# Two decoder blocks in one kernel: gate and up as seven block products, and the down products spread between the tiles of the next group

## Chip, cores and metric

The kernel runs on one core of one Trainium2 chip. The metric is the device time in microseconds (us), the median of the runs. Engines: PE (TensorE matmul) with its weight loads PEld, DVE (VectorE), ACT (ScalarE), POOL (GpSimd), SP (the queue that issues loads).

## The reference

The input is x, 512 tokens by 1024 features, in fp32. The model is a chain of six phases: FFN, even mixer, FFN, FFN, odd mixer, FFN. The change is in the four FFNs:

```python
h = rms_norm(x, ffn1_norm[i])
x = x + 0.5 * swiglu(h, w_gate, w_up, w_down)

def swiglu(x, w_gate, w_up, w_down):      # 1024 -> 2816 -> 1024
    return (jax.nn.silu(x @ w_gate) * (x @ w_up)) @ w_down
```

The even mixer is a gated linear recurrence beside block attention; the odd mixer is a 31-tap convolution beside attention on selected keys. Both end in an output product that is added to x.

## The kernel before

x lies in SBUF transposed, as 8 tiles `xt` of 128 features x 512 tokens. Each fp32 operand of a product is cut in two: `hi` is the value rounded to fp32r by ACT, `lo` the rest, subtracted by DVE. A product is three matmuls: hi x hi, lo x hi, hi x lo (L546 to L548, one per block of 128 rows). A **unit** is a weight tile of up to 8 blocks, loaded by SP into one of 4 `raw` slots, split by ACT (L947) into `w_hi` and by DVE (L1350) into `w_lo`, each with two buffers, so that a unit is split while the one ahead of it is multiplied. Its sum of 8 x 3 matmuls of 512 columns goes to one of two banks `ps_unit`.

An FFN has 22 tiles of 128 hidden features. A tile takes two units, gate and up. DVE scales gate by the norm's `rstd` (L1396), ACT takes silu (L967), DVE multiplies up with it (L1403), ACT and DVE cut the result into `a_hi` (L971) and `a_lo` (L1407). After each group of tiles (`GROUPS` = 8, 8, 6) come 8 **down units**, one per tile of x, each with 3 matmuls for each hidden tile of the group; DVE scales each by half of `rstd` (L1429) and adds it to x (L1431). During the last group's down units, and during the last output units of a mixer (`mix_out`, L1712), ACT and DVE already cut the new x into `xs_hi` and `xs_lo` (L1358) and sum its squares into `acc` (L1367). PE waits for `xs_lo` block by block in the first unit of a phase; the sum of squares becomes `rstd` during the first two units (L591, L597).

The order on each engine is that of the code; FFN loops are hardware loops on PE, ACT, DVE and SP. DVE's code for a pair of tiles before:

```python
gate(n + 2 * m, (n0 + 2 * m) % 2, tile + m)
lo_ahead(n + (2 * m + 2), 2 * m + 2, n0)
up(n + (2 * m + 1), (n0 + 2 * m + 1) % 2, tile + m)
lo_ahead(n + (2 * m + 3), 2 * m + 3, n0)
hidden_lo(j + m, tile + m)
```

## Time and profile before

| | |
|---|---|
| time, median of 3 runs | 1999.82 us (1998.88 to 1999.99) |
| span of the profiled execution, first to last instruction | 1996.9 us |
| mean granted TensorE clock | 0.997 of full |
| PE, PEld, DVE, ACT, POOL busy | 1968.5, 1613.8, 1076.8, 771.1, 50.0 us |
| matmuls | 9054 |
| moved by DMA | 213.80 MB, 107 GB/s |

The profiled execution has no timed result of its own; its span lies 2.9 us below the median of the three runs. Busy time of PE is the time in which any matmul is under way; a matmul's own duration contains its way through the array, so that neighbours overlap, and the spacing of their starts is what one costs. PE is busy for 99% of the span.

### The profile page before, as it was taken

Reading aid. Unit: us, or ns where it says so; the run is one execution under the profiler, and the core shown is the slowest. Engines: PE = TensorE matmul, PEld = TensorE weight load, DVE = VectorE, ACT = ScalarE, POOL = GpSimd, SP = SyncE. Lnnn points to the kernel's source line nnn. Section 1 sums busy time; section 2 is a strip of 40 time slices with the busy share of each in tenths; the row PEclk is TensorE's granted clock in tenths of the full one; section 3 lists DMA queues with packets and bytes.
Section 4 is the critical chain, followed back from the end, with each engine's and each line's share of the span. In section 5 each row is a group of like instructions: output and inputs, shape, how many; then the busy total and the mean of one; then the engine's idle time right before and its main releaser. Section 6 shows DMA issues by size and latency. Waiting matters only on the chain.

```text
span 1996.9 us, 25404 instructions
## 1 busy us (share of the span) xinstructions
PE 1968.5 (99%) x9054; PEld 1613.8 (81%) x9054; DVE 1076.8 (54%) x1673; ACT 771.1 (39%) x1110; POOL 50.0 (3%) x86
## 2 busy tenths in 40 slices
PE   7999999999999999999999999999999999999999
PEld 5888888888778888888888888877778778888887
DVE  5444444767674444446544444456989854444444
ACT  4222222477773222224332222354555852223222
POOL 1000000000000000000000000011111000000000
PEclk9999999999999999999999999999999999999999
DMA  4254433321122222233322233267765352332223
GB/s 166 101 122 121 137 96 100 110 74 64 55 84 95 95 95 96 99 100 105 106 95 95 95 96 102 96 163 168 158 153 133 87 137 96 97 103 95 95 95 105
DMA packets 60863, 213.80 MB, mean 107 GB/s; under 512 B 6616, under 2 KB 6872, under 8 KB 60792
## 3 DMA queue, kind: packets, MB, share of 16 engines
q1 hardware_dynamic: 52080, 184.97, 28.2%
q0 software_dynamic: 6192, 22.55, 6.2%
q10 hardware_dynamic: 2520, 5.36, 1.5%
q8 instruction: 43, 0.70, 0.1%
q14 instruction: 28, 0.23, 0.0%
HBM read 185.32 MB, written 4.72 MB: 95 GB/s over the span
## 4 chain that ended last, share of the span: by engine, by line
PE 89%; DVE 6%; ACT 3%; issue 2%; DMA 0%; SPq 0%; DVEq 0%; ACTq 0%
PE ps_unit L546 28%; PE ps_unit L548 28%; PE ps_unit L547 28%; DVE cv L1795 1%; DVE isc L1776 1%; PE ps_t L675 1%; DVE top L1774 1%; PE ps_s L546 1%; PE ps_y L547 0%; PE ps_y L548 0%; ACT w_hi L947 0%; PE ps_y L546 0%; PE ps_misc L636 0%; ACT L962 0%; DVE pt_lo L1543 0%
## 5 line engine op out<-in xcount | busy, mean ns | idle before, releaser
L947 ACT ACTIVATE w_hi<-raw 128x1024 fp32r<-128x1024 f32 x301 | 319.2, 1061 | 1019.9 <-PE ps_unit L548 1009.8
L546 PE MATMUL ps_unit<-xs_hi,w_hi 128*128 128x512 f32 x1768 | 697.3, 394 | 11.9 <-DVE xs_lo L1358 11.1
L547 PE MATMUL ps_unit<-xs_lo,w_hi 128*128 128x512 f32 x1768 | 688.9, 390 | 0.0
L548 PE MATMUL ps_unit<-xs_hi,w_lo 128*128 128x512 f32 x1696 | 660.9, 390 | 0.0
L1350 DVE TENSOR_TENSOR w_lo<-raw,w_hi 128x1024 fp32r<-128x1024 f32 x301 | 368.1, 1223 | 84.4 <-ACT w_hi L947 84.3
L546 PEld LDWEIGHTS ps_unit<-xs_hi,w_hi 128*128 128x128 f32 x1768 | 332.3, 188 | 87.8 <-DVE w_lo L1350 9.3
L547 PEld LDWEIGHTS ps_unit<-xs_lo,w_hi 128*128 128x128 f32 x1768 | 332.6, 188 | 68.5 <-issue 1.7
L548 PEld LDWEIGHTS ps_unit<-xs_hi,w_lo 128*128 128x128 f32 x1696 | 318.8, 188 | 66.9
L546 PE MATMUL ps_unit<-a_hi,w_hi 128*128 128x512 f32 x892 | 350.4, 393 | 2.4 <-DVE t L1472 0.8
L547 PE MATMUL ps_unit<-a_lo,w_hi 128*128 128x512 f32 x892 | 347.5, 390 | 0.0
L548 PE MATMUL ps_unit<-a_hi,w_lo 128*128 128x512 f32 x845 | 329.2, 390 | 0.0
L1403 DVE TENSOR_TENSOR t<-ps_unit,t 128x512 f32<-128x512 f32 x88 | 60.9, 692 | 276.7 <-PE ps_unit L548 276.7
L546 PEld LDWEIGHTS ps_unit<-a_hi,w_hi 128*128 128x128 f32 x892 | 167.7, 188 | 40.3 <-issue 2.1
L547 PEld LDWEIGHTS ps_unit<-a_lo,w_hi 128*128 128x128 f32 x892 | 167.7, 188 | 33.9
L548 PEld LDWEIGHTS ps_unit<-a_hi,w_lo 128*128 128x128 f32 x845 | 158.6, 188 | 33.4
L1396 DVE TENSOR_TENSOR t<-ps_unit,rstd 128x512 f32<-128x512 f32 x88 | 60.9, 692 | 217.2 <-PE ps_unit L548 217.0
L1429 DVE TENSOR_TENSOR t<-ps_unit,half 128x512 f32<-128x512 f32 x96 | 66.4, 692 | 196.1 <-PE ps_unit L548 191.3
L1431 DVE TENSOR_TENSOR xt<-xt,t 128x512 f32 (+1 forms) x96 | 66.5, 692 | 10.8 <-DVE t L1429 6.5
L930 ACT ACTIVATE w_hi<-raw 128x1024 fp32r<-128x1024 f32 x43 | 45.5, 1058 | 57.1 <-PE ps_unit L548 52.8
L1407 DVE TENSOR_TENSOR a_lo<-t,a_hi 128x512 f32 (+1 forms) x88 | 60.2, 684 | 0.0
L967 ACT ACTIVATE t<-t 128x512 f32<-128x512 f32 x88 | 54.1, 615 | 11.1 <-DVE t L1396 11.1
L971 ACT ACTIVATE a_hi<-t 128x512 f32 (+1 forms) x88 | 55.1, 627 | 0.2 <-issue 0.2
(236 smaller groups left out, 1292.6 us busy)
## 6 DMA issues: line engine op xcount, KB each, us to landing
raw<-w_stream_dram SPq DMA_DIRECT2D x344, 512.0 KB, 3.5
w_lo<-raw POOLq DMA_DIRECT2D x28, 512.0 KB, 5.2
w_lo_3rd<-raw POOLq DMA_DIRECT2D x15, 512.0 KB, 5.3
skew<-table ACTq DMA_DIRECT2D x1, 2560.0 KB
bias_t<-skew ACTq DMA_DIRECT2D x1, 2048.0 KB, 9.7
out_dram<-xt SPq DMA_DIRECT2D x8, 256.0 KB, 2.0
xt<-xt_in_dram SPq DMA_DIRECT2D x7, 256.0 KB, 6.0
bd_raw<-bd_in_dram SPq DMA_DIRECT2D x1, 512.0 KB, 8.1
```

The source lines that it names most:

```text
L546: pe.matmul(ps, lhs_hi, rhs_hi, start=first, stop=False)
L547: pe.matmul(ps, lhs_hi, rhs_lo, start=False, stop=False)
L548: return pe.matmul(ps, lhs_lo, rhs_hi, start=False, stop=last)
L947: act.activation(w_hi[:, s, :], raw[:, slot, :], ACT.Copy).then_inc(w_hi_done, 1)
L967: act.activation(t1[:, :], t0[:, :], ACT.Silu).then_inc(silu_done, 1)
L971: act.activation(a_hi[:, ds(j * T, T)], t2[:, :], ACT.Copy).then_inc(a_hi_done, 1)
L1350: dve.tensor_tensor(w_lo[:, s, :], raw[:, slot, :], w_hi[:, s, :].bitcast(F32), ALU.subtract).then_inc(w_lo_done, 1)
L1396: dve.tensor_tensor(t0[:, :], ps_unit[:, s, :], rstd[:, :], ALU.mult).then_inc(unit_read, 1)
L1403: dve.tensor_tensor(t2[:, :], ps_unit[:, s, :], t1[:, :], ALU.mult).then_inc(unit_read, 1)
L1407: dve.tensor_tensor(a_lo[:, ds(j * T, T)], t2[:, :], a_hi[:, ds(j * T, T)].bitcast(F32), ALU.subtract).then_inc(a_lo_done, 1)
L1429: dve.tensor_tensor(t0[:, :], ps_unit[:, s, :], half[:, :], ALU.mult).then_inc(unit_read, 1)
L1431: dve.tensor_tensor(xt_tile(d), xt_tile(d), t0[:, :], ALU.add).then_inc(x_added, 1)
```

## The change

**Gate and up of a hidden tile become one product of 2 x 2 blocks.** The blocks of weights are gate and up for the even and for the odd tiles of x (512 rows x 128 each); the blocks of x are its even and odd tiles, each for the first and the last 256 tokens. Seven block products in place of eight, each of 4 row blocks x 3 matmuls of 256 columns, give the same four results; three of them go one after the other into one bank, `chain`, which ACT copies out after each. Sums and differences ahead of and behind the products come with it. For weights: pieces of `gu` come by `gu_load` (five transfers of 256 KB in three DMAs), two sums are made by adding DMAs of POOL (`sums`), two by DVE (`second_sum`, `fourth_sum`), and the seven pieces are cut by `gw_high` and `gw_low`. For x: `split_u` makes the seven pieces (an even tile: `even_x`; an odd tile: `odd_x`) in place of `split_x`. The squares of x are no longer summed beside it, but in the first tile of an FFN (`squares_of_x`). Behind: `gate`, `gate_normed`, `up`, `gated`, `hidden_lo` on DVE, one product of a tile (`gate_right`) and all of that running a tile late.

**Groups are 4, 4, 4, 4, 6 tiles.** Down units of the first four groups no longer stand together: two of them follow each tile of the next group (`BETWEEN`), and the last group's stand together at the end (`ENDS`). The number of their matmuls is the same. Down units are loaded, split and multiplied at the group's width.

**Also:** FFN code is written out without hardware loops; the bias table of the mixers goes through 16 DMAs of ACT's queue in place of one; the even mixer's block weights are loaded and cut inside that mixer.

The groups and where their down units stand:

```diff
-GROUPS = (8, 8, 6)
+GROUPS = (4, 4, 4, 4, 6)
...
+SPREAD = 2
...
+ENDS = {GROUP_AT[g + 1] - 1: g for g in range(len(GROUPS)) if not SPREAD or g == len(GROUPS) - 1}
+BETWEEN = {j: [] for j in range(-1, FT)}
+for _g in range(len(GROUPS) - 1 if SPREAD else 0):
+    for _u in range(KT):
+        BETWEEN[GROUP_AT[_g + 1] + _u // SPREAD].append(_g * KT + _u)
```

PE, one tile (`gu_product` is 12 matmuls; `first` is j = 0, `more` is j > 0):

```diff
+                gu_product(chain, 0, *of_u(0, 0), True, landed(ua_done))
...
+                gu_product(block_bank(r, 2), 1, *of_u(0, 1), True)
+                pe.wait_ge(gw_lo_done, split_count(f, 1))
+                pe.wait_ge(copy_done, 3 * f + 1)
+                gu_product(chain, 2, *of_xu(1), False, landed(uc_done))
+                if j == 1:
+                    pe.wait_ge(diag_done, i + 1)
+                    pe.matmul(ps_misc[:, :], ones[:, :], diag[:, :], start=True, stop=True).then_inc(rbc_done, 1)
+                if more:
+                    gate_right(f - 1)
+                else:
+                    a12_u2()
+                pe.wait_ge(gw_lo_done, split_count(f, 2))
+                pe.wait_ge(copy_done, 3 * f + 2)
+                gu_product(chain, 3, *of_xu(0), False)
+                gu_product(block_bank(r, 1), 4, *of_xu(2), False)
+                if more:
+                    a12_u2()
+                if first:
+                    pe.wait_ge(const_done, 2)
+                    pe.wait_ge(acc_done, KT * (i + 1))
```

PE, behind a tile, the last group and the others:

```diff
+                    if j in ENDS:
+                        g, u0 = ENDS[j], ENDS[j] * KT
+                        before = GROUPS[g] - 1
...
+                        down_part(i, u0, range(before))
+                        gate_right(f)
...
+                        down_part(i, u0 + 1, range(before))
+                        for u in (u0, u0 + 1):
+                            down_part(i, u, [before]).then_inc(unit_done, 1)
+                        for u in range(u0 + 2, u0 + KT):
+                            down_unit(i, u)
+                    for u in BETWEEN[j]:
+                        down_unit(i, u)
```

DVE, one tile:

```diff
+            def hidden(f, j, i, more):
+
+                if not split_ahead(j):
+                    gw_low(f, 2)
+                    gw_low(f, 3)
+                    fourth_sum(f)
+                if j == 1:
+                    norm_diag(i)
+                if more:
+                    gw_low(f + 1, 0)
+                for u in BETWEEN[j - 1]:
+                    down(i, u)
+                    dve.wait_ge(x_added, X_BASE[i] + u + 1)
+                if j == 0:
+                    squares_of_x(i)
+                if pended(j):
+                    gate(f - 1)
+                    if j == 1:
+                        norm_rstd(i)
+                    gate_normed(f - 1)
+                if not split_ahead(j):
+                    gw_low(f, 4)
+                if more:
+                    second_sum(f + 1)
+                if pended(j):
+                    gated(f - 1)
+                if more:
+                    gw_low(f + 1, 1)
+                if pended(j):
+                    hidden_lo(f - 1, j - 1)
+                up(f)
```

ACT, one tile:

```diff
+                chain_copy(f, 1, sqb[:, r, 0:TH])
+                if not split_ahead(j):
+                    gw_high(f, 3)
+                if more:
+                    gw_high(f + 1, 0)
+                chain_copy(f, 6, sqb[:, r, TH:T])
+                if j == 0:
+                    squares_of_x(i)
+                if not split_ahead(j):
+                    gw_high(f, 4)
+                for u in BETWEEN[j - 1]:
+                    n = UNIT_BASE[i] + u + 2
+                    split_hi(n, n % RAW, n % 2)
+                if f:
+                    act.wait_ge(up_done, f)
+                chain_copy(f, 7, diag[:, 0:TH])
+                if pended(j):
+                    gate_silu(f - 1)
+                if more:
+                    gw_high(f + 1, 1)
+                if pended(j):
+                    hidden_hi(f - 1, j - 1, i)
+                if more:
+                    gw_high(f + 1, 2)
```

DVE, an odd tile of x for an FFN (an even one takes one subtraction of 256 columns and one `lo` of 512):

```diff
+                dve.scalar_tensor_tensor(scr[:, 3, :], x[:, TH:T], g, s[:, 2, :], ALU.mult, ALU.subtract).then_inc(u76_done, 1)
+                dve.wait_ge(u76_done, 2 * n - 1)
+                dve.scalar_tensor_tensor(scr[:, 4, :], scr[:, 3, :], -1.0, s[:, 0, :], ALU.mult, ALU.subtract).then_inc(u76_done, 1)
+                dve.wait_ge(u76_done, 2 * n)
+                dve.scalar_tensor_tensor(scr[:, 5, :], x[:, 0:TH], g, scr[:, 4, :], ALU.mult, ALU.add).then_inc(u4_done, 1)
```

The loads of weights for a tile, with the wait that is queued ahead of the later ones on SP:

```diff
+                sp.dma_start(gu[:, 8 + r, :], gu_stream[f, 0][:, 1, :]).then_inc(gu_landed[r], 16)
...
+                sp.wait_ge(gu_landed[r], 48 * (f // 2) + 16)
+                for part in range(2):
+                    sp.dma_start(gu[:, 4 * r + 2 * part:4 * r + 2 * part + 2, :], gu_stream[f, part]).then_inc(gu_landed[r], 16)
```

Three places in the order of instructions. The first is **DVE in one tile**. Before, these five rows are one hidden tile (`t_65` is gate, `t_67` is the product of gate and up):

```order
L1396 TENSOR_TENSOR t_65<-ps_unit,rstd 128x512 [waits silu_done,unit_done]
L1350 TENSOR_TENSOR w_lo<-raw,w_hi 128x1024 [waits w_hi_done]
L1403 TENSOR_TENSOR t_67<-ps_unit,t_66 128x512 [waits a_hi_done,silu_done,unit_done]
L1350 TENSOR_TENSOR w_lo<-raw,w_hi 128x1024 [waits w_hi_done]
L1407 TENSOR_TENSOR a_lo<-t_67,a_hi 128x512 [waits a_hi_done]
```

After, these are the second half of the tile j = 8 of an FFN, the first tile behind the group 4 to 7. The rows L1926 to L1740 are `down` of a unit of the group 0 to 3, L1863 to L1887 finish tile 7, the last row is `up` of tile 8:

```order
L1926 TENSOR_TENSOR t_65<-ps_unit,half 128x512 [waits x_added,unit_done]
L1928 TENSOR_TENSOR xt<-xt,t_65 128x512 [waits unit_read]
L1740 TENSOR_TENSOR w_lo<-raw,w_hi 128x512 [waits w_hi_done]
L1863 TENSOR_TENSOR t_65<-sqb,ps_t 128x512 [waits copy_done,silu_done,prod_done,x_added]
L1868 TENSOR_TENSOR t_65<-t_65,rstd 128x512 [waits gate_done]
L1839 TENSOR_TENSOR gw_lo<-gu,gw_hi 128x512 [waits gw_hi_done]
L1848 TENSOR_TENSOR gu<-gu 128x512 [waits gw_lo_done,gu_landed1,s1_landed]
L1883 TENSOR_TENSOR t_67<-t_67,t_66 128x512 [waits silu_done,up_done]
L1839 TENSOR_TENSOR gw_lo<-gu,gw_hi 128x512 [waits gw_hi_done]
L1887 TENSOR_TENSOR a_lo<-t_67,a_hi 128x512 [waits a_hi_done]
L1878 TENSOR_TENSOR t_67<-diag,ps_s 128x512 [waits a_hi_done,a_lo_done,copy_done,prod_done]
```

The `a_lo` of a tile now stands behind the down work, and in the tile after its own.

The second place is **PE where down units begin**. Before, the last gate and up loop ends, and the loop of down units begins:

```order
L548 MATMUL ps_unit<-xs_hi,w_lo 128x512
L616 REGISTER_ALU
L616 COMPARE_AND_BRANCH
L620 UNCONDITIONAL_BRANCH
L620 ISA
L563 REGISTER_ALU [waits w_lo_done]
L546 MATMUL ps_unit<-a_hi,w_hi 128x512 [waits a_lo_done,unit_read]
L547 MATMUL ps_unit<-a_lo,w_hi 128x512
L548 MATMUL ps_unit<-a_hi,w_lo 128x512
L546 MATMUL ps_unit<-a_hi,w_hi 128x512 [waits a_lo_done]
L547 MATMUL ps_unit<-a_lo,w_hi 128x512
L548 MATMUL ps_unit<-a_hi,w_lo 128x512
```

After, in tile j = 8, the last two matmuls of its last product are followed by the first unit of the group 4 to 7; each third matmul waits for one tile's `a_lo`, and the last row here for that of tile 7:

```order
L812 MATMUL ps_s<-xs_lo,gw_hi 128x256
L813 MATMUL ps_s<-xs_hi,gw_lo 128x256
L747 MATMUL ps_unit<-a_hi,w_hi 128x512 [waits a_lo_done,unit_read,w_lo_done]
L748 MATMUL ps_unit<-a_lo,w_hi 128x512
L749 MATMUL ps_unit<-a_hi,w_lo 128x512
L747 MATMUL ps_unit<-a_hi,w_hi 128x512 [waits a_lo_done]
L748 MATMUL ps_unit<-a_lo,w_hi 128x512
L749 MATMUL ps_unit<-a_hi,w_lo 128x512
L747 MATMUL ps_unit<-a_hi,w_hi 128x512 [waits a_lo_done]
L748 MATMUL ps_unit<-a_lo,w_hi 128x512
L749 MATMUL ps_unit<-a_hi,w_lo 128x512
L747 MATMUL ps_unit<-a_hi,w_hi 128x512 [waits a_lo_done]
```

Before, the down units stand behind the up product of the group's last tile; now they stand behind the seven products of the tile after it.

The third place is **DVE at the end of the even mixer**. Before, the last tile of x, and the split of the FFN's second unit:

```order
L1712 TENSOR_TENSOR xt<-xt,ps_unit 128x512 [waits unit_done]
L1350 TENSOR_TENSOR w_lo<-raw,w_hi 128x1024 [waits w_hi_done]
L1358 SCALAR_TENSOR_TENSOR xs_lo<-xt,vec,xs_hi 128x512 [waits x_hi_done,unit_read]
L1367 TENSOR_TENSOR acc<-acc,sqb 128x512 [waits acc_done,sq_done]
L1350 TENSOR_TENSOR w_lo<-raw,w_hi 128x1024 [waits w_hi_done]
```

After, the last tile of x up to the first sum of squares; the rows L1774 to L1786 are `odd_x` and `odd_x_lo`, and L1839 is `gw_low`:

```order
L2226 TENSOR_TENSOR xt<-xt,ps_unit 128x512 [waits unit_done]
L1740 TENSOR_TENSOR w_lo<-raw,w_hi 128x512 [waits w_hi_done]
L1774 SCALAR_TENSOR_TENSOR scr<-xt,vec,scr 128x256 [waits uc_done,unit_read]
L1776 SCALAR_TENSOR_TENSOR scr<-scr 128x256 [waits u76_done]
L1778 SCALAR_TENSOR_TENSOR scr<-xt,vec,scr 128x256 [waits u76_done]
L1783 SCALAR_TENSOR_TENSOR xs_lo<-xt,minus_gain,xs_hi 128x512 [waits ub_hi_done]
L1786 TENSOR_TENSOR xu_lo<-scr,xu_hi 128x768 [waits uc_hi_done]
L1839 TENSOR_TENSOR gw_lo<-gu,gw_hi 128x1024 [waits gw_hi_done]
```

Two operations for a tile of x became five for an odd one (and two for an even one), with the cut of weight pieces among them.

## Rows read from the trace of the kernel before

**Rows 1.** The page: busy time of the engines, and the chain that ended last.

```profile
PE 1968.5 (99%) x9054; PEld 1613.8 (81%) x9054; DVE 1076.8 (54%) x1673; ACT 771.1 (39%) x1110; POOL 50.0 (3%) x86
PE 89%; DVE 6%; ACT 3%; issue 2%; DMA 0%; SPq 0%; DVEq 0%; ACTq 0%
```

**Rows 2.** Window of a steady stretch: engines' busy us (x instructions), clock, DMA share, GB/s.

```profile
200.00:300.00 100.00, 100.00 (x443) 82.81 (x442) 42.51 (x50) 24.41 (x28) 0.00 (x0) 1.00 0.35 117
```

**Rows 3.** Waits of PE: total us, times, longest.

```profile
PE ps_unit L546 <- DVE xs_lo L1358: 11.1, 5, 9.4
```

**Rows 4.** Timeline of PE in the even mixer: start us, duration us.

```profile
455.81 0.28 PE L546 MATMUL ps_y<-pt_hi,v_hi 128*128 128x256 f32 x1
455.93 0.28 PE L547 MATMUL ps_y<-pt_lo,v_hi 128*128 128x256 f32 x1
...
456.40 0.28 PE L548 MATMUL ps_y<-pt_hi,v_lo 128*128 128x256 f32 x1
456.51 0.22 PE L546 MATMUL ps_y<-pt_hi,v_hi 128*128 128x128 f32 x1
```

**Rows 5.** Timeline of the weight loads in the same stretch.

```profile
455.81 0.19 PEld L547 LDWEIGHTS ps_y<-pt_lo,v_hi 128*128 128x128 f32 x1
455.93 0.19 PEld L548 LDWEIGHTS ps_y<-pt_hi,v_lo 128*128 128x128 f32 x1
```

**Rows 6.** Groups by form: busy us, mean ns | idle before.

```profile
L1429 DVE TENSOR_TENSOR t<-ps_unit,half 128x512 f32<-128x512 f32 x96 | 66.4, 692 | 196.1 <-PE ps_unit L548 191.3 <-issue 4.8
L1519 DVE SCALAR_TENSOR_TENSOR probs_more<-ps_s,hinv,isc 128x256 f32<-128x256 f32 x8 | 3.8, 477 | 0.0
L947 ACT ACTIVATE w_hi<-raw 128x1024 fp32r<-128x1024 f32 x301 | 319.2, 1061 | 1019.9 <-PE ps_unit L548 1009.8 <-DMA raw<-w_stream_dram 9.8
L967 ACT ACTIVATE t<-t 128x512 f32<-128x512 f32 x88 | 54.1, 615 | 11.1 <-DVE t L1396 11.1
L967 ACT ACT_TABLE_LOAD x4 | 5.1, 1283 | 0.1
L1029 ACT ACTIVATE v_hi<-ps_misc 128x256 fp32r<-128x256 f32 x16 | 5.1, 369 | 1.6 <-PE ps_misc L644 1.6
```

**Rows 7.** Timeline of DVE, end of the even mixer and start of the next FFN.

```profile
577.05 0.69 DVE L1712 TENSOR_TENSOR xt<-xt,ps_unit 128x512 f32<-128x512 f32 x1 [2.92 <-PE ps_unit L548]
...
588.43 1.22 DVE L1350 TENSOR_TENSOR w_lo<-raw,w_hi 128x1024 fp32r<-128x1024 f32 x1
...
592.10 0.68 DVE L1712 TENSOR_TENSOR xt<-xt,ps_unit 128x512 f32<-128x512 f32 x1
592.70 1.22 DVE L1350 TENSOR_TENSOR w_lo<-raw,w_hi 128x1024 fp32r<-128x1024 f32 x1
593.83 0.75 DVE L1358 SCALAR_TENSOR_TENSOR xs_lo<-xt,vec,xs_hi 128x512 fp32r<-128x512 f32 x1
...
596.66 0.69 DVE L1712 TENSOR_TENSOR xt<-xt,ps_unit 128x512 f32<-128x512 f32 x1 [1.48 <-PE ps_unit L548]
...
598.96 0.74 DVE L1358 SCALAR_TENSOR_TENSOR xs_lo<-xt,vec,xs_hi 128x512 fp32r<-128x512 f32 x1
```

**Rows 8.** Timeline of the first 20 us.

```profile
4.84 1.28 ACT L947 ACT_TABLE_LOAD   x1 [4.84 <-DMA raw<-w_stream_dram]
...
8.47 0.74 DVE L1358 SCALAR_TENSOR_TENSOR xs_lo<-xt,vec,xs_hi 128x512 fp32r<-128x512 f32 x1
...
9.36 0.76 PE L546 MATMUL ps_unit<-xs_hi,w_hi 128*128 128x512 f32 x1 [9.36 <-DVE xs_lo L1358]
...
20.23 0.94 PE L591 MATMUL ps_misc<-ones,acc 128*128 128x1 f32 x8
```

**Rows 9.** DMA issues: count, KB, median us to landing.

```profile
raw<-w_stream_dram SPq DMA_DIRECT2D x344, 512.0 KB, 3.5
w_lo<-raw POOLq DMA_DIRECT2D x28, 512.0 KB, 5.2
```

**Rows 10.** One DMA issue on ACT's queue, duration ns.

```profile
L1172 ACTq DMA_DIRECT2D bias_t<-skew x1: 406/406/406, 237.1 to 237.1; - x1
```

More of the change, by code:

```diff
@@ L21 @@
 FT = DFF // P
-GROUPS = (8, 8, 6)
+GROUPS = (4, 4, 4, 4, 6)
+GROUP_AT = [sum(GROUPS[:g]) for g in range(len(GROUPS) + 1)]
+SPREAD = 2
+A_SLOTS = 8
 UNIT = KT * P
@@ L46 @@
 SKEW = 640
-FFN_UNITS = 2 * FT + len(GROUPS) * KT
+COPIES = 8
+FFN_UNITS = len(GROUPS) * KT
+PAIRS = KT // 2
+TH = T // 2
+PIECE = PAIRS * P
 EVEN_IN = 5
@@ L540, in _, with ffn @@
                     add_raw(n)
+            def ffn(i):
+                for f in range(FFN_BASE[i], FFN_BASE[i + 1]):
+                    sums(f)
+                    if f == 1:
+                        softplus_first()
+                    if f == GROUPS[0] + 1:
+                        softplus()
+            for i, phase in enumerate(PHASES):
+                {"ffn": ffn, "even": even, "odd": odd}[phase](i)
         @block.tensor
@@ new lines, in gu_product @@
+            def gu_product(ps, piece, hi, lo, first, wait=None):
+                for j in range(PAIRS):
+                    if wait:
+                        wait(j)
+                    w = slice(j * P, (j + 1) * P)
+                    pe.matmul(ps, gw_hi[:, piece, w], hi(j), start=first and j == 0, stop=False, skip_group_check=True)
+                    pe.matmul(ps, gw_hi[:, piece, w], lo(j), start=False, stop=False, skip_group_check=True)
+                    mm = pe.matmul(ps, gw_lo[:, piece, w], hi(j), start=False, stop=j == PAIRS - 1, skip_group_check=True)
+                mm.then_inc(prod_done, 1)
@@ L680, in weigh @@
                 pe.wait_ge(pt_lo_done, 8 * a + 4 * half + 4)
+                if half == 0 and a % 4 == 0:
+                    pe.wait_ge(const_done, 6 + 4 * (a // 4 + 1))
                 if half == 0 and a < 4:
@@ L1405, in hidden_lo @@
[L1405 to L1422 removed]
+                dve.tensor_scalar(half[:, :], rstd[:, :], -0.5, None, ALU.mult).then_inc(half_done, 1)
@@ new lines, in down @@
+            def down(i, u):
+                n = UNIT_BASE[i] + u
+                add_down(n, n % 2, u % KT, X_BASE[i] + u)
+                if n + 2 < NUNITS:
+                    split_lo(n + 2, (n + 2) % RAW, (n + 2) % 2)
+            def ffn(i):
+                ffn_next = i + 1 < len(PHASES) and PHASES[i + 1] == "ffn"
+                for j in range(FT):
+                    f = FFN_BASE[i] + j
+                    hidden(f, j, i, j + 1 < FT or ffn_next)
+                    if f == 1:
+                        dve.wait_ge(sp_done, 1)
+                        dve.reciprocal(sp[:, 8:12], sp[:, 12:16]).then_inc(sp_inv_done, 1)
+                    if j not in ENDS:
+                        continue
+                    more = j + 1 < FT or ffn_next
+                    if more:
+                        gw_low(f + 1, 2)
+                        gw_low(f + 1, 3)
+                        fourth_sum(f + 1)
+                    gate(f)
+                    gate_normed(f)
+                    gated(f)
+                    hidden_lo(f, j)
+                    if more:
+                        gw_low(f + 1, 4)
+                    for u in range(ENDS[j] * KT, ENDS[j] * KT + KT):
+                        down(i, u)
+                        if j == FT - 1 and i + 1 < len(PHASES):
+                            dve.wait_ge(x_added, X_BASE[i] + u + 1)
+                            next_x(i + 1, u % KT)
+                    dve.wait_ge(x_added, X_BASE[i] + ENDS[j] * KT + KT)
```

717 lines of the change are left out of this document (494 added, 223 removed).

## The prediction

> **What bounds the kernel now.** I read the page first: PE is busy 1968.5 of 1996.9 us, and 89% of the chain that ended last is PE [rows 1]. So time goes only with PE's work, or with its waits. The window 200 to 300 us shows the steady FFN: 443 matmuls in 100 us without a gap, 0.2257 us each, while DVE works 42.5 us and ACT 24.4 [rows 2]. The list of waits shows how little PE waits: 11.1 us for `xs_lo`, of which 9.4 are the start of the program [rows 3]. The page's PE share tells that waits are nearly absent; the reader is to see that a change which takes work off PE and lays it on DVE (42% used) trades against something that is free now.
>
> **What is removed.** Gate and up take 48 matmuls of 512 columns a tile, 48 x 0.2257 = 10.83 us. After, 7 products of 12 matmuls of 256 columns. The trace has such matmuls, each with a new weight load, in the even mixer: from 455.81 to 456.51, six starts, 0.1167 us each [rows 4]. 84 x 0.1167 = 9.80 us. A product is 1.40. The gain is 1.03 a tile, 88 tiles: **-90.6 us**. It is smaller than an eighth, since narrow matmuls cost more a column.
>
> A weight load lasts 0.19 us, longer than the spacing of 0.1167, and the next one starts 0.12 later [rows 5]: loads overlap each other. The Trainium skill, "TensorE: Matmul & The Clock Gate", section "LDWEIGHTS (loading the stationary operand)", gives a load columns / 1.2 ns, 107 ns for 128, as much as 256 columns need; and its section "Back-to-back issue gap" lets both set the spacing. Laid end to end they would double a product and the change would lose hundreds of us (a rival below, priced from rows); laid side by side, by that page's 262 cycles against 518, the gain would be 104 us and the sum 2023. The trace agrees with side by side, and its own spacing is used.
>
> Down matmuls keep number and width: 0. Code without loops: 0, since the mixers are written out too and hold 0.1167 [rows 4]; that a long run does so no row shows, and it is in the range with the late weights.
>
> **Prices of what is added.** DVE, start to start: 0.60 us for 512 columns, 1.13 for 1024 [rows 7], by interpolation 0.87 for 768; 0.48 for 256 [rows 6]; 0.72 where the next instruction reads the result of one of 0.69. ACT: 1.06 for 1024, about 0.62 for 512, 0.37 for 256 from PSUM, a table load 1.28 [rows 6]. A hand-off to another engine: 0.15 (DVE's end at 8.47 + 0.74, PE's start at 9.36) [rows 8]; I take 0.05 to 0.2.
>
> **Steady tiles.** DVE's 12 operations of a tile sum to 2 x 1.13 + 10 x 0.60 + 0.12 = 8.4 us against 9.80 of PE. With two down units it has 12.4 (2 x (0.72 + 0.60 + 0.68) more) against 9.80 + 24 x 0.2257 = 15.2. ACT has 2 x 1.06 + 5 x 0.62 + 3 x 0.37 = 6.3, and 7.6 with two unit cuts. So PE paces both kinds, if nothing in a tile waits in a ring. I laid out one tile with down units, 0 being the start of its first product: products end at 1.4, 2.8, 4.2, 5.6 (the late gate of the tile before), 7.0, 8.4, 9.8. ACT copies `chain` at 1.6, so that its next weight cut is done at 2.55 and DVE's at 3.2; DVE sums to 3.8; ACT's cut after the second product ends at 4.05, DVE's at 5.25; two `down` to 9.5 (they wait for `split_hi`, which ACT reaches at 6.35 behind the fourth product); then gate 10.2, normed 10.8, cut 11.4, sum 12.0, gated 12.65, cut 13.4, `a_lo` 14.1. What PE needs of this in the next tile is there in time. Without down units DVE is at `gate` at 5.8 and at `a_lo` at 10.3. No term for steady tiles: DVE's cover is 1.4 us (no down units) and 2.8 (with them); if it is gone, each us costs 88.
>
> **Seams.** Six terms.
>
> 1. Tile 8, 12, 16 of each FFN. PE comes to the first down unit of the finished group at 9.8, to its fourth block at 9.8 + 9 x 0.2257 = 11.8, and needs the `a_lo` that DVE makes behind two `down` at 14.1. **2.3 us x 12 = +28.** Tile 4 has no `down` ahead of it, `a_lo` at 10.3 is in time. Bounds: 0 if DVE were not held up by `down`, 4 x 12 = 48 if each hand-off costs 0.2.
> 2. The end of each FFN. PE does 15 matmuls, the last gate product, 15 more (3.4 us) and waits for the chain gate, normed, silu, gated, `a_hi`, `a_lo`: 0.72 + 0.7 + 0.7 + 0.75 + 0.7 + 0.7 = 4.3 and hand-offs: 1.05 late. Then units 0 and 1 end together, and unit 2's `w_lo` stands on DVE behind the drain of unit 0: 0.1 + 0.72 + 0.6 + 0.87 less 0.65 since unit 0's end: 1.75 late. **2.8 x 4 = +11.**
> 3. x for an FFN behind a mixer. DVE needs for a pair of x tiles: even 0.5 + a wait for ACT 0.7 + 0.6 = 1.8; odd 3 x 0.5 + 0.66 + 0.3 of waiting + 0.87 = 3.4. Four pairs 20.8, weight cuts and sums of the first tile 5.3, adding x 4.8, unit cuts 4.6, some waits: 36 us from 577.05 on, so 613. Before, the last `xs_lo` ends at 599.7, and PE leaves the mixer at 596.66 [rows 7]. PE can do P1, P5 and three quarters of the third product, 3.9 us, before it needs the last odd tile: 613.3 - 600.5 = 12.8. The odd mixer's tail has the same list. **2 x 13 = +26** (bounds 2 x 8 and 2 x 18: an idle PE also loses granted clock).
> 4. FFN to FFN: a pair costs DVE 5.2 and its two down units 2 x (0.72 + 0.6 + 0.75), 9.3 to 10, against 36 x 0.2257 = 8.1 of PE: 1.5 us late at each second unit, then 2.2 and 2.5 at the last even and odd tile, **+8** beside term 2.
> 5. First two tiles of each FFN. Eight squares on ACT and seven adds on DVE (0.6 to 0.75 each) begin when the last x piece is cut and end 8.4 us later; PE ends its tile at 5.2 and waits 3.2. In the second tile the chain root (with 1.28 of table load), diag, `rstd` costs 1.05, 1.4 and 0.4. **6 x 4 = +24** (bounds 3 and 9 each).
> 6. The start of the program. Before, PE starts at 9.36 and has done 24 matmuls at 20.23 [rows 8]; with the sums of squares (0.94) and a second unit (5.4) tile 0 ends near 27. After: a first piece (landing 3.5 us or less [rows 9]), then 1 MB, land near 10; table load (it stands at 4.84 now, behind the first landing [rows 8]), cut and four even tiles at 1.85: 19.3; cuts of the other pieces to 25.3; four odd tiles at 3.4 and one cut: 39.5; the third product ends there, and three more at 44.1. Tile 0 is 8.4 us of PE now, 10.8 before: (44.1 - 8.4) - (27 - 10.8) = 20, and 2 for clock: **+22**.
>
> Smaller: 16 issues of 0.41 us each [rows 10] on ACT at the end of tile 15, 6.5 us, of which 4 reach PE: **+4**. PE's idle stretches of over 3 us at seams 3 and 6 will show a lower granted clock: **+5**.
>
> DMA: a tile loads 1.5 MB and adds 0.25 MB in SBUF. Landing is 3.5 us for 512 KB, 5.2 for an adding one [rows 9]; behind the wait on SP the chain is 3.5 + 5 to 7 + 5, some 15 us, with two buffers and so 19.6 us for it: hidden.
>
> **Sum:** 1996.9 - 90.6 + 28 + 11 + 26 + 8 + 24 + 22 + 4 + 5 = 2034; the span lies 2.9 us below the median, so **2037 us**.
>
> **Rivals.**
> *Preparation of x is hidden* (faster). Terms 3, 4 and 6 are one mechanism, the ring ACT, DVE, ACT, DVE over x pieces, 56 us. If ACT runs ahead and DVE's short operations close up, it is gone, and 1981 comes out. It decides where the 56 shrink to 19, or a pair of x tiles to under 3 us on DVE; for it, that DVE is at 42% [rows 2]; against, that at 592.10 to 596.66 DVE is full as it is [rows 7], and odd tiles double that.
> *Weights of a tile come late.* SP waits for a first piece to land before it issues the other two, POOL adds behind both. If a tile's pieces are 1 us behind its cut, 88 us more: 2125. For it: the adding transfers and four landings in a row; against: two buffers.
> *Weight loads do not overlap when they never pause.* 84 x 0.19 = 15.96 a tile, 6.16 over the forecast, x 88: 2579. Rows 5 speak against it.
> *No effect*: gain and seams cancel, 2000.
>
> **Chances.** Forecast 0.58 (its own range 2010 to 2065), x hidden 0.20, late weights 0.17, loads in line 0.02, no effect 0.03. Range 1985 to 2100: below it half of the x case, above it the large losses. 0.2% of the time is about what a measurement of this kernel tells from no change. Faster 0.20, same 0.05, slower 0.75 (forecast, and both costlier rivals, less 0.02 near zero).
>
> **What would show it.** PE in a steady FFN: about 857 starts of 256 columns in 100 us where no down units stand, no idle; DVE 85% busy there. In tile 8 a wait of 2 to 2.5 us in the first down unit, for `a_lo`. Near 597 to 613 PE idle for some 13 us, for `xs_lo` and `xu_lo`. At the start a first matmul near 14, the tile done near 44. Wrong it would be if the spacing of 256 columns is not 0.117 under steady load, if DVE's steady tile is longer than PE's, or if seams are half as long.

## Result and profile after

The changed kernel takes 2071.6 us (median of 4 runs, 2069.2 to 2074.3), the kernel before 1999.6 in the same rounds: ratio 1.036, 95% interval 1.0345 to 1.0375, so slower by 3.6%. The time lies in the range given (1985 to 2100), 35 us above the point and 7 above the forecast case's own range.

The page of the profiled execution of the kernel after, the lines that answer to [rows 1]:

```profile
span 2072.5 us, 32930 instructions
PE 1926.4 (93%) x12222; PEld 1722.9 (83%) x12222; DVE 1583.5 (76%) x2558; ACT 1038.3 (50%) x1735; POOL 208.8 (10%) x267
PE 74%; DVE 14%; ACT 5%; issue 5%; DMA 1%; ACTq 1%; DVEq 0%; POOL 0%; SPq 0%; POOLq 0%
```

PE's busy time fell from 1968.5 to 1926.4 us, and its idle time (span less busy) rose from 28.4 to 146.1: 117.7 more. The chain that ended last now runs 14% through DVE (6% before). The mean granted clock of the four runs was 0.973 to 0.981; the profiled run, read here, is the one with 0.973 and the longest of them, 2.7 us above the median.

Two windows of the kernel after, against [rows 2]. 60 to 88 us holds tiles without down units, 120 to 150 mostly tiles with two:

```profile
core 0: us, PE busy (x) PEld busy (x) DVE busy (x) ACT busy (x) POOL busy (x), PEclk, DMA share, GB/s
60.00:88.00 28.00, 28.00 (x235) 27.02 (x234) 24.99 (x37) 18.20 (x29) 5.22 (x6) 1.00 0.62 162
120.00:150.00 30.00, 30.00 (x213) 28.09 (x211) 24.93 (x36) 14.00 (x26) 3.48 (x4) 1.00 0.61 158
```

PE has no gap in either. DVE is at 89% in the first (85% foretold). So the steady state holds, and the loss is elsewhere. What a tile costs shows in PE's timeline of the kernel after (start, duration), first a tile with two down units, then one without:

```profile
100.53 0.28 PE L811 MATMUL ps_y<-xs_hi,gw_hi 128*128 128x256 f32 x1
...
110.41 0.40 PE L747 MATMUL ps_unit<-a_hi,w_hi 128*128 128x512 f32 x1
...
115.88 0.28 PE L811 MATMUL ps_y<-xs_hi,gw_hi 128*128 128x256 f32 x1
```

```profile
76.90 0.28 PE L811 MATMUL ps_t<-xs_hi,gw_hi 128*128 128x256 f32 x1
...
86.66 0.28 PE L811 MATMUL ps_s<-xs_hi,gw_hi 128*128 128x256 f32 x1
```

84 product matmuls take 110.41 - 100.53 = 9.88 us in the first, 0.1176 each, and 24 down matmuls 5.47. In the second, 84 take 86.66 - 76.90 = 9.76 us, 0.1162 each. Foretold were 9.80 and 0.1167 [rows 4]. The gate and up units of a tile in PE's timeline of the kernel before:

```profile
170.46 0.39 PE L546 MATMUL ps_unit<-xs_hi,w_hi 128*128 128x512 f32 x1
...
181.34 0.39 PE L546 MATMUL ps_unit<-xs_hi,w_hi 128*128 128x512 f32 x1
```

These are 48 matmuls in 10.88 us, 0.2267 each. The prediction had 0.2257 and 10.83: it divided 100 us by the 443 matmuls of [rows 2], a number that counts those under way at the window's edges too; 441 start in it. With 16 tiles of each FFN followed by down units and 6 not, the gain is 64 x (10.88 - 9.88) + 24 x (10.88 - 9.76) = 91 us.

What PE waited for in the kernel after, the answer to [rows 3] (total, times, longest):

```profile
PE ps_y L811 <- ACT sqb L1306: 35.0, 6, 16.5
PE ps_unit L747 <- DVE a_lo L1887: 32.5, 16, 2.4
PE ps_y L811 <- DVE xs_lo L1766: 25.0, 7, 14.2
PE ps_misc L865 <- DVE acc L1807: 13.4, 4, 3.5
PE ps_unit L747 <- DVE w_lo L1740: 12.6, 8, 2.8
```

By seam, from the single stretches of idle time in PE's timeline (us, tiles counted from 0):

| seam | foretold | measured |
|---|---|---|
| 1, tiles 8, 12, 16: `a_lo`, 12 x 2.39 | 28 | 28.7 |
| 2, end of each FFN: 0.93 and 1.68, 4 times | 11 | 10.4 |
| 3, x behind the mixers: 9.3 and 10.0 | 26 | 19.3 |
| 4, FFN to FFN, beyond seam 2 | 8 | 6.2 |
| 5, first tiles: 3.08, 3.25, 3.52, 3.52 | 24 | 13.4 |
| 6, program start | 22 | 21.6 |
| bias DMAs at 287 us | 4 | 6.5 |
| tile 21 of each FFN, its third product: 3.0, 4 times | not seen | 12.0 |
| sum | 123 | 118 |

The sum comes out, in part by luck: seams 3 and 5 are 17 us less than foretold, and the unforeseen waits of tile 21 put 12 back. What remains is 2072.5 - 1996.9 + 91 - 117.7 = 49 us by which PE is busy longer than its matmuls need at full speed. The prediction had 5, for the clock. The mean clock is 0.973, and since the level is either 1.2 or 2.4 GHz, 2 x (1 - 0.973) = 5.4% of the span, 112 us, was at the half one. The clock of the trace, stretch by stretch, says the same: 19 stretches, 112.6 us in all, and PE is busy in 87.8 of them; before, 2 stretches, 10.2 us, with PE busy in 9.5. Half of the added busy time is the price: (87.8 - 9.5) / 2 = 39 us. Some 10 of the 49 us are the edges of the waits, an estimate from the lines below: in the record a matmul ahead of a wait is busy for 0.39 us and not 0.23, the first behind it takes 0.33, so that a wait adds 0.26 us of busy time, and there are 64 in place of 23. One half-level stretch, in PE's timeline of the kernel after, behind the wait of tile 8:

```profile
158.29 0.39 PE L749 MATMUL ps_unit<-a_hi,w_lo 128*128 128x512 f32 x1
161.07 0.50 PE L747 MATMUL ps_unit<-a_hi,w_hi 128*128 128x512 f32 x1 [2.39 <-DVE a_lo L1887]
161.40 0.39 PE L748 MATMUL ps_unit<-a_lo,w_hi 128*128 128x512 f32 x1
...
162.33 0.61 PE L749 MATMUL ps_unit<-a_hi,w_lo 128*128 128x512 f32 x1
162.74 0.63 PE L747 MATMUL ps_unit<-a_hi,w_hi 128*128 128x512 f32 x1
163.17 0.63 PE L748 MATMUL ps_unit<-a_lo,w_hi 128*128 128x512 f32 x1
...
165.30 0.60 PE L747 MATMUL ps_unit<-a_hi,w_hi 128*128 128x512 f32 x1
165.73 0.41 PE L748 MATMUL ps_unit<-a_lo,w_hi 128*128 128x512 f32 x1
```

PE is idle 2.39 us, runs on at full speed for a while, and then eight matmuls take 0.43 us each in place of 0.2267: 1.6 us more. The same wait at 771.03 left the clock whole, as windows of the two show:

```profile
158.00:166.00 8.00, 5.61 (x18) 4.12 (x18) 4.61 (x7) 2.44 (x4) 1.01 (x2) 0.79 0.54 110
770.00:778.00 8.00, 6.97 (x44) 6.32 (x45) 3.58 (x6) 2.39 (x5) 0.87 (x1) 1.00 0.35 68
```

Six of the twelve waits of this kind met such a dip, and each of the 19 half-level stretches begins inside an idle stretch of PE or at most 1.3 us behind one. That the dips come from the waits is so far only a reading; the experiments test it.

### The profile page after: what moved, and what is told of

Its sections match the earlier page's. It is cut to its first block, busy times and chain, and to the rows that moved or that the text cites. A ratio compares the mean times of both kernels' runs of the same rounds, so it can differ in the third digit from the quotient of the medians.

```text
span 2072.5 us, 32930 instructions
## 1 busy us (share of the span) xinstructions
PE 1926.4 (93%) x12222; PEld 1722.9 (83%) x12222; DVE 1583.5 (76%) x2558; ACT 1038.3 (50%) x1735; POOL 208.8 (10%) x267
## 3 DMA queue, kind: packets, MB, share of 16 engines
q0 software_dynamic: 31536, 68.70, 19.3%
## 4 chain that ended last, share of the span: by engine, by line
PE 74%; DVE 14%; ACT 5%; issue 5%; DMA 1%; ACTq 1%; DVEq 0%; POOL 0%; SPq 0%; POOLq 0%
PE ps_unit L747 11%; PE ps_unit L748 10%; PE ps_unit L749 10%; PE ps_y L811 6%; PE ps_y L813 6%; PE ps_y L812 6%; PE ps_t L811 4%; PE ps_t L813 4%; PE ps_t L812 4%; PE ps_s L811 3%; PE ps_s L813 3%; PE ps_s L812 3%; DVE w_lo L1740 1%; DVE gw_lo L1839 1%; DVE t L1926 1%
## 5 line engine op out<-in xcount | busy, mean ns | idle before, releaser
L1839 DVE TENSOR_TENSOR gw_lo<-gu,gw_hi 128x512 fp32r<-128x512 f32 (+1 forms) x439 | 394.3, 902 | 208.7 <-ACT gw_hi L1302 200.6
L1302 ACT ACTIVATE gw_hi<-gu 128x512 fp32r<-128x512 f32 (+1 forms) x439 | 349.1, 798 | 205.6 <-PE ps_s L813 68.7
L811 PE MATMUL ps_y<-xu_hi,gw_hi 128*128 128x256 f32 x704 | 201.8, 287 | 39.1 <-ACT sqb L1306 35.0
L813 PE MATMUL ps_y<-xu_hi,gw_lo 128*128 128x256 f32 x704 | 200.6, 285 | 0.0
L812 PE MATMUL ps_y<-xu_lo,gw_hi 128*128 128x256 f32 x704 | 200.3, 285 | 0.0
L1740 DVE TENSOR_TENSOR w_lo<-raw,w_hi 128x512 fp32r<-128x512 f32 (+2 forms) x189 | 153.8, 814 | 31.4 <-ACT w_hi L1231 31.4
L811 PE MATMUL ps_s<-xs_hi,gw_hi 128*128 128x256 f32 x528 | 151.5, 287 | 0.0
L811 PE MATMUL ps_t<-xs_hi,gw_hi 128*128 128x256 f32 x528 | 149.9, 284 | 0.0
L812 PE MATMUL ps_s<-xs_lo,gw_hi 128*128 128x256 f32 x528 | 149.4, 283 | 0.0
L812 PE MATMUL ps_t<-xs_lo,gw_hi 128*128 128x256 f32 x528 | 149.2, 283 | 0.0
```

Source lines behind the costliest of these rows:

```text
L811: pe.matmul(ps, gw_hi[:, piece, w], hi(j), start=first and j == 0, stop=False, skip_group_check=True)
L812: pe.matmul(ps, gw_hi[:, piece, w], lo(j), start=False, stop=False, skip_group_check=True)
L813: mm = pe.matmul(ps, gw_lo[:, piece, w], hi(j), start=False, stop=j == PAIRS - 1, skip_group_check=True)
L1302: act.activation(gw_hi[:, w, :], src, ACT.Copy).then_inc(gw_hi_done, 1)
L1740: dve.tensor_tensor(w_lo[:, s, w], raw[:, slot, w], w_hi[:, s, w].bitcast(F32), ALU.subtract).then_inc(w_lo_done, 1)
L1839: dve.tensor_tensor(gw_lo[:, w, :], src, gw_hi[:, w, :].bitcast(F32), ALU.subtract).then_inc(gw_lo_done, 1)
```

## Experiments

Theory A: the loss is PE's idle time at seams and the half clock that follows some of it. B: narrow matmuls or the written-out code cost it. C: the clock falls without regard to idle time. D: spreading down units between tiles is the loss beyond its own waits. "Tile 21" is the last of an FFN, in the expectations too. "Idle" below is span less PE busy, "clock" the granted mean of the profiled run; the kernel after has 146.1 and 0.973. Times "off" are from the median of the kernel after, 2071.6. The cuts of code are shortened at "...".

**e1_shift**: down units one tile later.

```
-        BETWEEN[GROUP_AT[_g + 1] + _u // SPREAD].append(_g * KT + _u)
+        BETWEEN[GROUP_AT[_g + 1] + 1 + _u // SPREAD].append(_g * KT + _u)
```

> Only the order on PE's, ACT's and DVE's lists changes: each group's down units begin one tile later (tiles 5 to 8, 9 to 12, 13 to 16, 17 to 20 after the first in place of 4 to 7 and so on), so that every a_lo is old when the first down unit needs it, and tile 20 has down units on PE as well as on ACT and DVE. Theory A (the loss is PE's idle time at the seams, with the half granted clock that follows some of it): the 12 waits of 2.39 us at tiles 8, 12 and 16 go (28.7 us), the dips of the granted clock behind six of them go (about 10 us), and the wait of tile 21, 3.0 us four times, shrinks or moves (6 us at most): 40 to 45 us off, 2027 to 2032. Theory B (narrow matmuls or the written-out code as such are the cost): nothing, 2072. Theory C (the granted clock falls without regard to idle time): the waits alone, 29 to 33 us off, about 2040, with the clock's mean still 0.973. Rival: another wait takes the place of the removed one, since the last down unit of a group now stands right ahead of the next group's end: under 15 us off, above 2057.

Measured 2033.3 us, ratio 1.0168 (1.0151 to 1.0185): 38.3 off, 1 us above A's range and 7 below C's 2040. Idle 118.2, clock 0.979. The 12 waits and the 4 of tile 21 are gone (40.7), others of 12.8 came. One of them is new in kind; PE's timeline, then ACT's, then POOL's of this kernel:

```profile
106.58 0.55 PE L811 MATMUL ps_y<-xu_hi,gw_hi 128*128 128x256 f32 x1 [6.06 <-ACT sqb L1306]
```

```profile
105.11 1.06 ACT L1302 ACTIVATE gw_hi<-gu 128x1024 fp32r<-128x1024 f32 x1 [7.74 <-DMA gu<-gu_stream_dram]
106.08 0.36 ACT L1306 ACTIVATE sqb<-ps_y 128x256 f32<-128x256 f32 x1
```

```profile
87.96 0.54 POOL L662 TENSOR_TENSOR sp<-sp 128x4 f32<-128x4 f32 x1
...
99.89 0.22 POOL L672 TENSOR_SCALAR c<-sp 128x4 f32<-128x4 f32 x1
100.77 0.93 POOL L693 DMA_DIRECT2D gu<-gu_stream_dram  x1 [0.65 <-POOL c L672]
```

PE waits for ACT's copy of the chain; ACT does that copy behind a cut that waits for an adding transfer; and POOL issues this transfer behind more than 12 us of small operations for the constants of the even mixer's recurrence. Under a tile with down units that was hidden. B falls: products and written-out code are all there, and 38 us went. The two profiled spans differ by 41.0 us: 27.9 are idle time, and 13.1 are PE busy time, with the same matmuls. Ten waits fewer are worth some 3 of these by the edges above; the others go with the clock, since PE is busy at the half level for 64.1 us in place of 87.8. C leaves that out.

**e2_filler**: matmuls whose result nobody reads fill the 12 waits.

```
+                for _ in range(10):
+                    pe.matmul(ps_misc[:, :], a_hi[:, at:at + P], a_hi[:, at:at + T], start=True, stop=True)
```

> Ten matmuls of 512 columns whose result nobody reads (a_hi times a_hi into the bank for small things) stand ahead of the last block of the first down unit at tiles 8, 12 and 16 of each FFN, where PE is idle for 2.39 us now. Ten at 0.2257 take 2.26 us. They fill the idle time and take nothing away from it. Theory A (half clock follows from idle PE): the waits are gone from the list or under 0.3 us each, the end of each stands where it was, and the dips of the granted clock behind six of them are gone: 5 to 12 us off, 2060 to 2067, mean clock 0.977 or more. Theory C (the clock falls without regard to idle time, by the load as such): no change or up to 3 us slower, and the same number of dips. If the waiting was not for a_lo at a fixed time but for PE's own progress, 12 x 2.26 = 27 us are added, 2099.

Measured 2065.5 us: 6.1 off; the runs of the two kernels do not overlap (2064.4 to 2067.7, against 2069.2 to 2074.3). Idle is 121.3. The four runs have clocks of 0.979 to 0.983, against 0.973 to 0.981, which alone would say little; but in the trace the 12 waits are gone, and none of its 13 half-level stretches stands at any of the 12 places, where the kernel after has six. No work was saved, only the idle time replaced by work, and the kernel is faster. C falls: the dips follow idle time.

**e3_products**: the seven block products alone, with groups of 8, 8, 6 and no down units between tiles.

```
-GROUPS = (4, 4, 4, 4, 6)
+GROUPS = (8, 8, 6)
-SPREAD = 2
+SPREAD = 0
```

> The seven block products alone, with the grouping of before: groups of 8, 8 and 6 tiles, each group's eight down units together at its end, three ends an FFN, no down units between tiles. Gone: 12 waits of 2.39 (28.7), 4 of tile 21 (12.0), some six dips of the clock behind them (10). Added: two more group ends an FFN, eight in all, at 2.6 us each (0.93 and 1.68, as at tile 21 of the kernel after) = 21, with some dips, 5. The matmuls are the same in number. DVE has no down drains under the tiles. Theory A: 2072 - 51 + 26 = 2047, range 2038 to 2058. Theory B (narrow matmuls or written-out code are the cost): 2072 +- 5 less nothing, since products stay. Theory D (spreading down units between tiles is the main loss, beyond its 51 us): clearly under 2035.

Measured 2051.9 us, ratio 1.0263 (1.0246 to 1.028), idle 130.5, clock 0.974. Within A's range: the new grouping costs the kernel 19.7 us against the products alone, close to the difference worked out from its own waits (51 less 26 in the expectation). D, which asked for clearly under 2035, falls.

**e4_bias**: the 16 bias DMAs, two in each of the tiles 12 to 19.

```
-                    if i == 0 and j in (7, 15):
-                        prepare(j // 8)
+                    if i == 0 and 12 <= j < 20:
+                        prepare(j - 11)
```

> The 16 DMA issues of the bias table leave the end of tile 15 of the first FFN, where ACT issues them all in a row, and are spread two to a tile over tiles 12 to 19. Theory A: PE's one wait of 6.45 us at 287 us goes, and the half clock from 285.2 to 292 with it (about 3 us): 6 to 10 us off, 2062 to 2066. Rival: the issues take 0.41 us each wherever they stand and ACT hands all of it on to PE: no change.

Measured 2062.2 us: 9.4 off, in the range. Idle is 139.6, 6.5 less, and the wait of 6.45 is gone. The twelve waits of 2.39 us are untouched here, and seven of them met a dip in place of six: which ones do differs from run to run.

**e5_ssq**: PE takes the sum of squares behind the second product of the second tile, 1/rms behind the fourth.

```
                 gu_product(block_bank(r, 2), 1, *of_u(0, 1), True)
+                if j == 1:
+                    pe.wait_ge(acc_done, KT * (i + 1))
...
```

> Only the seam between the first and the second tile of each FFN is changed: PE takes the sum of squares over partitions (four small matmuls) behind the second product of the second tile in place of the end of the first, and the matmul that spreads 1/rms behind that tile's fourth product; ACT takes the square root behind its next copy and cut; SP issues the third tile's gate and up load before two waiting unit loads. Theory A: the four waits for acc, 13.4 us in all, shrink to under 1 us each (acc is ready 3.5 us after the first tile, two products are 2.8), and most of the half clock behind them (6.8 us at half speed, four times, some 3.4 us of PE each) goes too: 15 to 25 us off, 2047 to 2057, mean clock 0.978 or more. Theory C (clock without regard to idle time): 10 to 13 us off. Rival: the later square root makes DVE late with normed and the wait comes back in the third tile: under 5 us off.

Measured 2070.5 us: 1.1 off, nothing, as the rival had it (under 5), though by another wait than the one it named. The waits of this kernel show which:

```profile
PE ps_y L814 <- ACT diag L1309: 10.5, 4, 2.9
```

The four waits for `acc`, 13.4 us, became four for ACT's third copy of the chain, 10.5. This copy stands behind eight squares in ACT's queue. That it had been nearly as late before, hidden behind the later wait, is so far argued; e9 to e11 test it. The prediction's account of seam 5, "PE waits for the sum of squares", named only the last of two.

**e6_end**: the last gate product ahead of the first down unit; DVE cuts the next weights between the two halves of a drain.

```
+                        gate_right(f)
                         start_unit(UNIT_BASE[i] + u0, is_first=UNIT_BASE[i] + u0 < 2)
                         down_part(i, u0, range(before))
-                        gate_right(f)
...
                 dve.tensor_tensor(t0[:, :], ps_unit[:, s, :], half[:, :], ALU.mult).then_inc(unit_read, 1)
+                if then:
+                    then()
```

> Only the end of each FFN is changed: PE takes the last gate product of tile 21 ahead of the first down unit and not between the first two, so that ACT and DVE can begin the last tile's gate 3.4 us earlier; and DVE cuts the next unit's weights between the two halves of a drain and not behind both. Theory A: the two waits at each end (0.93 for a_lo, 1.68 for w_lo) shrink to under 0.3 and to about 1.0: 1.3 to 1.6 us four times, 5 to 7 us off, 2065 to 2067. Rival: DVE reaches the gate later than PE gives it, so that the a_lo wait stays and only 2 us come off.

Measured 2107.6 us: 36 slower, a clear miss. The waits of this kernel, and DVE's timeline in the last down tile ahead of tile 8's wait:

```profile
PE ps_unit L747 <- DVE a_lo L1887: 38.6, 12, 3.2
...
PE ps_t L811 <- DVE t L1878: 6.1, 4, 2.1
```

```profile
150.25 0.68 DVE L1926 TENSOR_TENSOR t<-ps_unit,half 128x512 f32<-128x512 f32 x1
151.99 0.69 DVE L1740 TENSOR_TENSOR w_lo<-raw,w_hi 128x512 fp32r<-128x512 f32 x1 [1.06 <-ACT w_hi L1231]
152.60 0.69 DVE L1930 TENSOR_TENSOR xt<-xt,t 128x512 f32<-128x512 f32 x1
```

The cut placed between the halves waits 1.06 us for ACT's `w_hi`, where before the add was done in that time: each of the 12 waits grew from 2.39 to 3.22. And the early gate product waits for `up` on DVE (L1878), which I had not followed. Idle time is 18.2 us more. PE is busy at the half level for 112.8 us in place of 87.8, worth 12.5: ten of the 12 longer waits met a dip, not six. Nine waits more are worth 2 by their edges. That is 33 of the 36 us; the rest stays open.

**e7_all**: e1, e4, e5 and e6 together.

> The four changes together: down units one tile later, bias DMAs spread, sum of squares in the second tile, the end's order. If each loss is a wait of its own, they add: measured -38.3 and -9.4, expected -20 and -6, from 2071.6: 1998, range 1988 to 2010, so about the time of the kernel before. If they share one budget (PE, once free here, waits there), it stays above 2015. The earlier gate product also meets the wait of 1.90 us for a_lo that the shift leaves at each end, and should take 1.4 off it.

Measured 2046.6 us, far above the range (1988 to 2010) and 13 above e1 alone. The end's order, a loss by itself, is in it. PE again waits for `up` at the end of each FFN; with the down units a tile later it is later too:

```profile
PE ps_t L814 <- DVE t L1884: 26.0, 4, 6.9
```

**e8_all**: e7, the first pieces issued together, the square root's table loaded ahead.

```
-                sp.wait_ge(gu_landed[r], 48 * (f // 2) + 16)
+                if f:
+                    sp.wait_ge(gu_landed[r], gu_all(f) - 32)
```

> As the run with all four changes, and two more: at the start of the program the first gate and up pieces are issued together, not one after the landing of the other, so that ACT's first cut, which stands at 9.24 us, begins near 5.5 to 6; and ACT loads the square root's table before it waits for the sum of squares (1.28 us of its chain, four times). Expected: 3 to 3.7 us off at the start, whose idle time is a fixed chain of x preparation, and 0 to 1 us at each second tile: 3 to 6 us below the run with all four. If the x landings are what the start waits for, nothing comes off.

Measured 2046.8 us, no difference to e7 (3 to 6 us were expected); in the trace PE's first matmul came at 12.41 in place of 13.64 us, a third of what was expected. What holds the start from there was not tried.

**e9_chain**: the queues of ACT and DVE in the first two tiles in another order (on the kernel after, without e6).

```
                 if j == 0:
+                    gw_high(f + 1, 1)
+                    squares_of_x(i, range(4))
...
                 chain_copy(f, 7, diag[:, 0:TH])
+                if j == 0:
+                    squares_of_x(i, range(4, KT))
```

> The last try moved the sum of squares on PE and the wait only changed its name: PE then waited 2.3 to 2.9 us for ACT's copy of the chain, which stands behind all eight squares, so that seam is ACT's and DVE's queue and not the reader of acc. Here that queue is changed: in the first tile of an FFN ACT copies the chain after four squares and cuts the fourth piece ahead of them; DVE makes the second sum and that cut first and the up subtraction ahead of the last two adds; PE's sum of squares stands behind the fourth product of the second tile, 1/rms behind the fifth; ACT loads the square root's table ahead. By this account the waits of 2.9 us go to under 1 us in all, and most of the half clock behind them: 12 us of idle time and 5 to 10 of clock, 2052 to 2058, against 2070.5 of the last try and 2071.6 of the kernel after. Rival: the seam is a matter of ACT's and DVE's sum of work in these two tiles (8 squares and 7 adds, 10 us on top), whatever the order: then the wait returns in the second or third tile and under 4 us come off.

Measured 2079.8 us: 8 slower, where 14 to 20 off were expected. PE's, ACT's and DVE's timelines of the second and third tile of the second FFN:

```profile
674.42 0.36 PE L814 MATMUL ps_y<-xu_hi,gw_hi 128*128 128x256 f32 x1 [3.59 <-ACT sqb L1311]
```

```profile
668.57 1.28 ACT L1317 ACT_TABLE_LOAD   x1
670.97 0.63 ACT L1317 ACTIVATE t<-t 128x512 f32<-128x512 f32 x1 [1.12 <-DVE t L1882]
672.43 0.63 ACT L1322 ACTIVATE a_hi<-t 128x512 fp32r<-128x512 f32 x1 [0.83 <-DVE t L1897]
672.96 1.04 ACT L1307 ACTIVATE gw_hi<-gu 128x1024 fp32r<-128x1024 f32 x1
673.91 0.36 ACT L1311 ACTIVATE sqb<-ps_y 128x256 f32<-128x256 f32 x1
```

```profile
663.22 0.18 DVE L1837 RECIPROCAL rcol<-small 128x4 f32<-128x4 f32 x1 [3.06 <-ACT small L1291]
```

The wait went one tile on, 3.59 us four times. It looks like the rival (too much work in these tiles), but the rows show room: DVE stands idle 3.06 us at the head of its queue with cuts behind it that could be done, and ACT's short copy stands behind a cut of 1.04 that PE does not need yet.

**e10_all**: e1, e4, the early first pieces, e9, and POOL's small operations one tile later (`if f == GROUPS[0] + 2`).

> Five changes together: down units one tile later (measured alone -38.3), bias DMAs spread (-9.4), the first and second tile's order (expected -15 to -20), the first pieces issued together at the start (-1.2 in the trace of the run with all), and POOL's thirteen us of small operations one tile later, under a tile with down units, so that the wait of 6.1 us that the shift uncovered at 106 us (the adding transfer stood behind them) goes, with its half clock: 6 to 9 us. The end's order is left as in the kernel after, since the change of it cost 36 us. If they add: 2071.6 - 38 - 9 - 17 - 1 - 8 = 1998, range 1992 to 2010. If the waits have a common cause (DVE's and ACT's work, 76% and 50% busy), above 2012.

Measured 2021.8 us, ratio 1.0112 (1.0095 to 1.0128), idle 110.6, clock 0.985: above the range (1992 to 2010). The wait at 106 is gone; the four of 3.59 that e9 brought are here too.

**e11_all**: e10 with the first two tiles ordered once more (the cut of code is e11 against e10); **e12_nochain**: e10 without any such order.

```
+                if j < 2:
+                    first_copy(f + 1)
...
-                    if j == 1:
-                        norm_diag(i)
                     gw_low(f, 3)
...
+                    act.activation(small[:, 7:8], small[:, 0:1], ACT.Silu)
```

> As the run of five changes, with the first two tiles ordered once more. There PE waited 0.6 to 1.2 us for ACT's first copy of the second tile (behind the squares and a cut of 1.04) and 3.59 us for that of the third (behind silu's table load, a_hi and a cut), while DVE had stood idle 3.06 us at its wait for the square root. Here both copies stand ahead of those cuts, silu's table is loaded ahead, and DVE does the cuts and the sum of the next tile in the time in which it stood idle. If the seam is an order of queues, both waits fall under 1 us: 4 x 3.9 = 15.6 us and some 10 us of clock off 2021.8: 1996, range 1991 to 2006. If it is the sum of work on ACT and DVE in these tiles, the wait moves on once more, to up of the second tile: under 6 us off, above 2015.

> The same without any change to the first two tiles: down units one tile later, bias DMAs spread, first pieces issued together, POOL's small operations one tile later. From 2071.6 less 38.3, 9.4, 1.2 and 6 to 9: 2014 to 2017. It stands beside the run of five changes (2021.8): if it is lower, that order of the first two tiles was a loss there too, as it was alone (2079.8 against 2070.5), by 4 x 1.5 us of waits or so.

Measured 1997.0 us for e11 (11 runs, 1995.4 to 1997.6), ratio to before 0.9988 (0.9979 to 0.9997), and 2014.8 for e12, ratio 1.0076. Both lie in their ranges. So the order in e10 was a loss of 7 us, and that of e11 is a gain of 17.8: seam 5 was an order of queues, not a sum of work. The page and the waits of e11:

```profile
span 1995.2 us, 32946 instructions
PE 1903.9 (95%) x12222; PEld 1705.3 (85%) x12222; DVE 1582.0 (79%) x2558; ACT 1036.8 (52%) x1743; POOL 209.3 (10%) x267
```

```profile
PE ps_y L821 <- DVE xs_lo L1794: 23.5, 7, 12.2
PE ps_y L821 <- ACT sqb L1318: 16.8, 3, 16.4
PE ps_unit L757 <- DVE w_lo L1768: 12.6, 8, 2.8
PE ps_unit L757 <- DVE a_lo L1921: 10.5, 8, 2.5
```

At this seam nothing waits for `acc` or `diag` any more beyond one wait of 0.95 us. Idle is 91.3 us, clock 0.984 (63 us at half level, PE busy in 44.9 of them). Against the kernel before: -91 of matmuls, +62.9 idle, (44.9 - 9.5) / 2 = 18 for the clock and 7 for the edges of 26 more waits. The sum is -3, and the span is 1.7 less. This version is 75 us faster than the kernel after. Against the kernel before its 0.1% is at the edge of what can be told.

## Why the prediction was right, and where it was off

- **Direction and mechanism**: right. PE works less and waits at seams, and steady tiles are paced by PE. The sum of the seams, 123 foretold, is 118; that it is so close is partly luck.
- **Gain**: 91 foretold and 91 measured, by errors that cancel. 48 matmuls of 512 columns take 10.88 us and not 10.83 (a misread count in [rows 2]), which is 4 us more to gain over 88 tiles. The 84 of 256 take 9.88 in the 64 tiles with down units and 9.76 in the others, not 9.80 throughout, 4 us the other way. The Trainium skill, "TensorE: Matmul & The Clock Gate", section "Back-to-back issue gap", has 262 cycles of 2.4 GHz for 256 columns, 109 ns; the trace has 116 to 118, with loads laid side by side as foretold.
- **Seams 1, 2, 4, 6**: within 2 us each. In term 2 the second half adds up to 1.64 and not the 1.75 written; 1.68 was measured. **Seam 3**: 19.3 for 26, and in another shape. No single idle stretch of 13 us came, but several of 0.5 to 5.4, in part for `w_lo` and `xt` in the mixer's last units; why it is less is not shown. **Seam 5**: 13.4 for 24. The second tile's waits did not come, and e5 and e9 to e11 show that even the first was misread: it was a copy behind the squares in ACT's queue as much as the sum itself.
- **Tiles 20 and 21**: missed, 12 us. I laid out tiles with and without down units, but not the one between: PE has none in tile 20, while ACT and DVE still do those of tile 19, and PE then waits in the third product of tile 21. e1, where tile 20 has down units on all three, removed it.
- **The step that failed** is "PE's idle stretches of over 3 us at seams 3 and 6 will show a lower granted clock: +5". Stretches of 2.39 us bring it too, half of the time, and nearly every seam adds its share: 39 us for the clock, and some 10 more for the edges of waits, for which the prediction had no term. e2 shows the clock's part with the wait filled (6.1 us off for no work saved, and no dip left at the twelve places). This makes the miss of the point: 49 in place of 5, less 5 of seams, is the 39 us between the 2034 worked out and the span of 2072.5.
- **Rivals**: x hidden (1981) did not come. e11's 1997 is no sign of it either: its waits for `xs_lo` are 23.5 us, against 25.0. Late weights did not come in the kernel after; e1 uncovered one such wait of 6.06 us, by POOL's queue and not by the landing of pieces. Loads in line: excluded by 0.1176.
